# A Strassen MLP on one core: GpSimd's accumulating DMAs moved in layer 0, four output products of each pair deferred into the next pair in layer 1

## The chip, the core and the metric

The kernel runs on one core of a Trainium2 chip. Its time is the device time of one launch in microseconds (us); the runs of the kernel before are given as their median. The core's engines are TensorE (PE; its weight loads are listed as PEld), VectorE (DVE), ScalarE (ACT), GpSimd (POOL) and SyncE (SP), which issues most DMAs. Each has its own queue, works it in order and waits on semaphores.

## The reference

Two layers over 1024 latent and 256 context tokens of width 1024. Layer 0 mixes tokens by a Fourier transform, layer 1 by windowed attention; each mixer is followed by a squared-ReLU MLP with 4096 hidden columns. The change touches the two MLPs alone.

```python
def _sq_relu_mlp(h, w1, w2):
    return jnp.square(jax.nn.relu(h @ w1)) @ w2
...
        h_lat = h_lat + g1 * y_lat
        h_lat = h_lat + g2 * _sq_relu_mlp(_modulate(_rms_norm(h_lat, norm2_g[i]), sh2, sc2), mlp_w1[i], mlp_w2[i])
```

## The kernel before

All matmuls are done in three passes on operands split into a high part (rounded, written by ScalarE) and a low part (what is left, `lo_part`, L58, written by DVE or GpSimd): high by high, low by high, high by low.

Each MLP runs over 16 **pairs** of hidden chunks of 128. In a pair, W1 makes four hidden blocks (B11, B12, B21, B22: two chunks by two halves of 512 tokens), the blocks are squared after ReLU, and W2 takes them back to 1024 rows, kept in `ht`. W2's product is made by Strassen's scheme: seven block products M1 to M7 instead of eight, each of 4 banks with 3 matmuls of 512 columns (12 matmuls). Their right operands are blocks or sums of blocks (T1 to T4), their left ones chunks of W2 or sums of them (S1 to S4). A product lands in four PSUM banks `y_ps` 0 to 3. DVE takes banks 0 to 2 (`acc`: ht += gate * bank). Bank 3 is the side bank: ScalarE copies it, scaled, to `side` (`side_read`), and GpSimd adds it to `ht` (`add`). A bank can be written by the next product only when it has been read.

**Layer 0** (`layer_tail`, L563). Hidden blocks are made directly; after them come M5, M3, M2, M1, M6, M7, M4, with small groups for the context tokens between them (256 columns, bank `l_yc_ps`). The next layer wants sums of its weights. They are made beside this loop, in DRAM: SP copies first terms to `sums` (L825 to L828), and four DMAs a pair on GpSimd's queue add the second terms: `first_sums` (L909, L910), which waits for SP's copies, and `more_sums` for S2 and for S4 (L922), S2 waiting for the first sums to have landed and S4 for S2. GpSimd's own work in a pair (`outputs`) is: addition M5, low part of S2 (of this layer's W2), addition M3, the first sums, the low part of the next pair's first W1 chunk (`low1`), the low part of S3, addition M2, the accumulation for S2, addition M1, the low parts of A22 and A21, the next W1 chunk, additions M6, M7, the accumulation for S4, addition M4. ScalarE splits the W1 chunk (L984, from `l_w1f`) between M1's and M6's side reads. DVE also adds up, from `l_aw`, a part of the modulation of layer 1 (L1288), which a small matmul reduces at the end of the hidden blocks (L1547).

**Layer 1** (`strassen_tail`, L1680). Here the hidden blocks are also made by seven products (M1, M5, M6, M2, M7, M3, M4 on banks `z_ps` 0 to 3, `hidden`), ScalarE copying three of them (`copied`) and DVE adding the copies (`zsum`). Pairs 0 and 1 are plain (hidden blocks directly; in pair 1 the inputs for the later pairs are summed and split, `low_t`); pairs 2 to 15 are alike, 2 to 14 in a loop. TensorE does the seven hidden products and then the seven output products M1, M6, M7, M4, M5, M3, M2. Between the two, DVE and ScalarE must turn hidden blocks into operands: ReLU, square, differences (`diff`), high part (`high`), low part (`low`). A product waits for its operand's low part, its weights' low part (`split2`) and, bank by bank, for the bank's last reader:

```python
                def pair(p):
                    for prod in Z_ORDER:
                        hidden(p, prod)
                    for i in (0, 1, 2, 3):
                        product(p, i)
```

Of the kernel before, what the change touches and what calls it, by code (L numbers as in the profile page):

```python
# [11 lines left out]
P = 128  # L12
# [550 lines left out]
def layer_tail(nc, sem, sb, banks, layer, wp, early, s_pw, w1, w2, mod, meanw, eps, ident, nh, nl, ht,  # L563
# [76 lines left out]
    with ExitStack() as ph:  # L640
# [125 lines left out]
        with nc.Block() as block:  # L766
# [97 lines left out]
            def _(pool):  # L864
# [60 lines left out]
                def outputs(p, more):  # L925
                    add(p, "M5")
                    low2(p, "S2")
                    add(p, "M3")
                    if C:
                        first_sums(p)  # L930
# [17 lines left out]
                    if more and not C:  # L948
                        low1(p + 1, 1)

# [26 lines left out]
                if C:  # L977
                    pool.wait_ge(s_s4, 16 * PAIRS)
# [701 lines left out]
def strassen_tail(nc, sem, sb, banks, wp, early, s_pw, w1, w2, sums, mod, meanw, eps, ident, nh, nl, nl_at, ht, park, out):  # L1680
# [12 lines left out]
    SIDE = 3  # L1693
# [25 lines left out]
    ON_DVE2 = 3  # L1719
    A_ORDER = ["B11", "T2", "T3", "T1", "T4", "B22", "B21"]  # L1720
    A_BUF = {"B11": 0, "B22": 0, "T2": 1, "B21": 1, "T3": 2, "T4": 3, "T1": 4}
    T_AT = {"T1": 1, "T2": 2, "T3": 3, "T4": 4}
    HOME_BANK = {"B21": 0, "B11": 1, "T4": 1, "T3": 2, "B22": 3}
    HOME_SLOT = {"T1": 0, "B12": 1, "T2": 3}
    RELU_SLOT = {"B11": 0, "B12": 1, "B22": 2, "B21": 2}
# [7 lines left out]
    with ExitStack() as ph:  # L1733
# [189 lines left out]
        def split2(eng, p, i):  # L1923
            if i < ON_DVE2:
                eng.wait_ge(s_w2d, p * ON_DVE2 + (PRE + i + 1))
            else:
                eng.wait_ge(s_w2p, p * (7 - ON_DVE2) + (PRE + i - ON_DVE2 + 1))

# [6 lines left out]
        with nc.Block() as block:  # L1935
            @block.sync
            def _(sp):
# [44 lines left out]
                for i in (4, 5, 6):  # L1982
                    load2(0, i, (0, i - 4))
# [5 lines left out]
                load2(1, 0, (0, 4))  # L1989
                load2(1, 1, (0, 5))  # L1990
                load1(2, 3, (1, 3))
                load2(1, 2, (0, 6))

                for i in (4, 5, 6):
                    load2(1, i, (1, i - 4))
                load1(2, 4, (2, 0))
                load1(2, 5, (2, 1))
                load2(2, 3, (1, 3))
                load1(2, 6, (2, 2))
                for i in (0, 1, 2):  # L2000
                    load2(2, i, (1, i + 4))

                with sp.Fori(PLAIN, PAIRS - 1) as p:
                    for i in (4, 5, 6):
                        load2(p, i, (p, i - 4))
                    load1(p + 1, 3, (p, 3))
                    load1(p + 1, 0, (p, 4))
                    load1(p + 1, 1, (p, 5))
                    load1(p + 1, 2, (p, 6))
                    load1(p + 1, 5, (p + 1, 1))  # L2010
                    load1(p + 1, 6, (p + 1, 2))
                    load1(p + 1, 4, (p + 1, 0))
                    load2(p + 1, 3, (p, 3))
                    for i in (0, 1, 2):
                        load2(p + 1, i, (p, i + 4))
                for i in (4, 5, 6):
                    load2(PAIRS - 1, i, (PAIRS - 1, i - 4))
# [9 lines left out]
            def _(pool):  # L2027
# [8 lines left out]
                def low2(p, i):  # L2036
                    pool.wait_ge(s_w2h, p * 7 + (PRE + i + 1))
                    lo_part(pool, w2l[:, i % 3], w2f[:, i % 4], w2h[:, i % 3]).then_inc(s_w2p, 1)

                def add(p, i):  # L2040
                    _, h = chunk(i, SIDE)
                    pool.wait_ge(s_ya, p * 7 + (PRE + i + 1))
                    pool.wait_ge(s_add, p * 7 + (PRE + i))
                    pool.tensor_tensor(h, h, side[i % 2][:], ALU.add).then_inc(s_add, 1)  # L2044
# [7 lines left out]
                def rest(p, more):  # L2052
                    if more:
                        low1(p + 1, 0)
# [1597 lines left out]
```

## Time and profile before

| | us |
|---|---|
| median of 3 runs | 2564.84 (2562.03 to 2565.29) |
| the profiled execution, its own time | 2568.6 |
| its span in the profile | 2567.1 |
| TensorE busy | 2319.5 (90%) |
| DVE busy | 1731.1 (67%) |
| ScalarE, GpSimd busy | 1155.4, 1155.5 (45% each) |

The layer-0 MLP's loop lies between about 410 and 1235 us of the span, the layer-1 MLP's pairs between about 1860 and 2550. Busy time of an engine is counted from instruction starts and ends; matmuls overlap, so TensorE's busy share is close to one also where it works below its pace. PEclk is the granted TensorE clock as a share of full speed. In the waits, the releaser is the operation whose semaphore came last.

### The profile page before, as it was taken

The page shows a single profiled execution, that of the slowest core. Times are in us where ns is not written, and L with a number is a line of the kernel's source. Part 1 is how long each engine was busy: PE and PEld are TensorE (multiplying, and loading weights), DVE is VectorE, ACT ScalarE, POOL GpSimd, SP SyncE. Part 2 cuts the span into 40 slices and gives each one's busy share as a digit, 9 for nine tenths or more (in the row PEclk, how much of TensorE's full clock was granted, in tenths as well). Part 3 has the DMA queues.
Part 4 walks back from the last instruction along what each step waited for, and adds up shares of the span by engine and source line. Part 5 has one row for each costly group of instructions (what it writes and reads, how often), then busy time and mean ns, then how long its engine had stood idle before and what let it go on. Part 6 is the DMA issues. An engine that isn't in the chain of part 4 may idle for free. (4 is left out here: it accounts for less than half of the span.)

```text
span 2567.1 us, 38476 instructions
## 1 busy us (share of the span) xinstructions
PE 2319.5 (90%) x11430; PEld 1908.2 (74%) x11430; DVE 1731.1 (67%) x2827; ACT 1155.4 (45%) x2117; POOL 1155.5 (45%) x974
## 2 busy tenths in 40 slices
PE   5989989999999999999789798989988999998988
PEld 3768768888888877888677677767767777777776
DVE  5643786766776766676674688871787676767675
ACT  5543433333333333333343488883444444444444
POOL 0004533333334444433546566665455554545453
PEclk9999989999999999999889899999989999999999
DMA  7434225555544555554512211105122222222222
GB/s 264 168 136 165 99 60 159 150 139 144 134 131 131 146 144 150 160 151 108 165 61 99 93 32 38 33 21 205 38 66 73 83 82 86 86 86 86 86 80 84
DMA packets 132197, 283.51 MB, mean 110 GB/s; under 512 B 11408, under 2 KB 19984, under 8 KB 128784
## 3 DMA queue, kind: packets, MB, share of 16 engines
q1 hardware_dynamic: 111776, 242.09, 28.1%
q0 software_dynamic: 17408, 33.56, 7.9%
q10 hardware_dynamic: 2928, 6.82, 0.7%
q8 instruction: 43, 0.70, 0.1%
q14 instruction: 42, 0.34, 0.0%
HBM read 265.64 MB, written 83.89 MB: 136 GB/s over the span
## 5 line engine op out<-in xcount | busy, mean ns | idle before, releaser
L881 POOL TENSOR_TENSOR ht<-ht,l_side 128x512 f32<-128x512 f32 x112 | 167.5, 1495 | 535.8 <-ACT l_side L1017 533.6
L51 PE MATMUL l_z_ps<-nh,l_w1h 128*128 128x512 f32 (+1 forms) x816 | 292.9, 359 | 6.6 <-POOL l_w1l L58 3.4
L53 PE MATMUL l_z_ps<-nh,l_w1l 128*128 128x512 f32 (+1 forms) x816 | 291.8, 358 | 0.0
L52 PE MATMUL l_z_ps<-nl,l_w1h 128*128 128x512 f32 (+1 forms) x800 | 285.8, 357 | 0.0
L1321 DVE SCALAR_TENSOR_TENSOR ht<-l_yy_ps,mod,ht 128x512 f32<-128x512 f32 x336 | 235.9, 745 | 20.6 <-PE l_yy_ps L1637 19.2
L2662 PE MATMUL l_yy_ps<-l_ah,l_w2h 128*128 128x512 f32 x448 | 190.2, 425 | 61.3 <-DVE ht L2491 61.1
L58 POOL TENSOR_TENSOR l_w2l<-l_w2f,l_w2h 128x512 fp32r<-128x512 f32 x128 | 181.4, 1467 | 108.9 <-ACT l_w2h L2157 105.1
L58 POOL TENSOR_TENSOR l_w1l<-early,l_w1h 128x512 fp32r<-128x512 f32 x104 | 135.6, 1311 | 179.7 <-ACT l_w1h L2149 179.7
L1635 PE MATMUL l_yy_ps<-l_ah,l_w2h 128*128 128x512 f32 x448 | 187.0, 417 | 22.3 <-ACT l_side L1017 14.6
L3389 POOL TENSOR_TENSOR sc<-sc,den 128x640 f32<-128x640 f32 (+1 forms) x128 | 149.5, 1200 | 91.8 <-DVE den L3471 91.8
L2664 PE MATMUL l_yy_ps<-l_ah,l_w2l 128*128 128x512 f32 x448 | 185.3, 414 | 0.0
L2663 PE MATMUL l_yy_ps<-l_al,l_w2h 128*128 128x512 f32 x448 | 185.3, 414 | 0.0
L1636 PE MATMUL l_yy_ps<-l_al,l_w2h 128*128 128x512 f32 x448 | 182.1, 407 | 0.0
L1637 PE MATMUL l_yy_ps<-l_ah,l_w2l 128*128 128x512 f32 x448 | 180.3, 402 | 0.0
L51 PEld LDWEIGHTS l_z_ps<-nh,l_w1h 128*128 128x128 f32 x816 | 154.8, 190 | 30.4 <-issue 4.0
L2044 POOL TENSOR_TENSOR ht<-ht,l_side 128x512 f32<-128x512 f32 x112 | 151.8, 1355 | 49.5 <-ACT l_side L2194 47.2
L1017 ACT ACTIVATE l_side<-l_yy_ps,mod 128x512 f32<-128x512 f32 x112 | 76.6, 684 | 214.8 <-PE l_yy_ps L1637 214.8
L53 PEld LDWEIGHTS l_z_ps<-nh,l_w1l 128*128 128x128 f32 x816 | 154.9, 190 | 22.4
L52 PEld LDWEIGHTS l_z_ps<-nl,l_w1h 128*128 128x128 f32 x800 | 152.0, 190 | 22.0 <-issue 0.5
L2662 PEld LDWEIGHTS l_yy_ps<-l_ah,l_w2h 128*128 128x128 f32 x448 | 90.1, 201 | 97.1 <-DVE ht L2491 58.4
L2491 DVE SCALAR_TENSOR_TENSOR ht<-l_yy_ps,mod,ht 128x512 f32<-128x512 f32 x192 | 136.3, 745 | 24.2 <-PE l_yy_ps L2664 24.2
L58 DVE TENSOR_TENSOR l_al<-l_slot,l_ah 128x512 fp32r<-128x512 f32 x144 | 119.8, 832 | 37.4 <-ACT l_ah L1010 34.2
(338 smaller groups left out, 6533.5 us busy)
## 6 DMA issues: line engine op xcount, KB each, us to landing
l_aw<-ada SPq DMA_DIRECT2D x128, 256.0 KB, 2.9
sums<-w SPq DMA_DIRECT2D x64, 512.0 KB, 7.8
maw<-ada SPq DMA_DIRECT2D x24, 1024.0 KB, 5.1
l_w1f<-w SPq DMA_DIRECT2D x32, 512.0 KB, 5.8
l_w2f<-w SPq DMA_DIRECT2D x32, 512.0 KB, 4.2
sums<-w POOLq DMA_DIRECT2D x32, 512.0 KB, 7.3
sums<-sums POOLq DMA_DIRECT2D x32, 512.0 KB, 5.9
l_w2f<-sums SPq DMA_DIRECT2D x64, 256.0 KB, 2.7
```

The costliest lines, as they stand in the source:

```text
L51: pe.matmul(out, lh, rh, start=first, stop=False)
L52: pe.matmul(out, lh, rl, start=False, stop=False)
L53: return pe.matmul(out, ll, rh, start=False, stop=last)
L58: return eng.tensor_tensor(lo, full, f32(hi), ALU.subtract)
L881: pool.tensor_tensor(h, h, side[(i - 1) % 2][:], ALU.add).then_inc(s_add, 1)
L1321: dve.scalar_tensor_tensor(out=h, in0=y_ps[m][:], scalar=mod[:, layer, G2, c, 0:1], in1=h, op0=ALU.mult, op1=ALU.add).then_inc(s_acc, 1)
L1635: pe.matmul(y_ps[m][:], wh, a_h, start=first, stop=False, skip_group_check=not first)
L1636: pe.matmul(y_ps[m][:], wh, a_l, start=False, stop=False, skip_group_check=not first)
L1637: pe.matmul(y_ps[m][:], wl, a_h, start=False, stop=True, skip_group_check=not first).then_inc(s_y, 1)
L2662: pe.matmul(y_ps[m][:], wh, a_h, start=start, stop=False, skip_group_check=not start)
L2663: pe.matmul(y_ps[m][:], wh, a_l, start=False, stop=False, skip_group_check=not start)
L2664: pe.matmul(y_ps[m][:], wl, a_h, start=False, stop=True, skip_group_check=not start).then_inc(s_y, 1)
```

## The change

**Layer 0.** GpSimd's four accumulating DMAs get other places in `outputs`. The first sums of pair p come first of all, behind the S4 accumulation of pair p − 1; S2's comes after the last addition. After the last pair S4's follows at once.

**Layer 1.** Output products 3 to 6 (M4, M5, M3, M2) of pair p − 1 are done among the hidden products of pair p: after hidden M1, M5, M6, and after the last one (M4). M1, M6, M7 of pair p follow. All five queues are rewritten to suit: the order of operands becomes B11, T2, T3, B21, T4, T1, B22; two low parts of W2 more are on DVE and fewer on GpSimd; copies and buffers change places; and of the first and the last output product (M1 and M2) two banks, 2 and 3, go by ScalarE and GpSimd instead of one. T2 and B21 share an operand buffer, as before, so the high part of T2 now waits for the output product M2 of the pair before.

```diff
                 def outputs(p, more):
+                    if C:
+                        if type(p) is not int or p:
+                            more_sums(p - 1, "S4")
+                        first_sums(p)
                     add(p, "M5")
                     low2(p, "S2")
                     add(p, "M3")
-                    if C:
-                        first_sums(p)
...
                     for prod in ROWS[2:]:
                         add(p, prod)
-                        if C and prod in ("M2", "M7"):
-                            more_sums(p, "S2" if prod == "M2" else "S4")
...
+                    if C:
+                        more_sums(p, "S2")
...
                 outputs(PAIRS - 1, False)
                 if C:
+                    more_sums(PAIRS - 1, "S4")
                     pool.wait_ge(s_s4, 16 * PAIRS)
...
-    A_ORDER = ["B11", "T2", "T3", "T1", "T4", "B22", "B21"]
+    A_ORDER = ["B11", "T2", "T3", "B21", "T4", "T1", "B22"]
+    A_AFTER = {"B11": (1, 5), "B22": (0, 0), "T2": (1, 6), "B21": (0, 1), "T1": (1, 4)}
+    SIDES = {i: [2, 3] if i in (0, 6) else [3] for i in range(7)}
...
-                def pair(p):
-                    for prod in Z_ORDER:
+                def pair(p, earlier=True):
+                    for k, prod in enumerate(Z_ORDER):
                         hidden(p, prod)
-                    for i in (0, 1, 2, 3):
+                        if earlier and k < 3:
+                            product(p - 1, 3 + k)
+                    if earlier:
+                        product(p - 1, 6)
+                    for i in (0, 1, 2):
                         product(p, i)
```

DVE's queue in a pair of layer 1, from the last difference on:

```diff
+                    diff(p, "T1")
+                    diff(p, "T2")
+                    if earlier:
+                        acc(p - 1, 6, (0, 1))
+                    square(p, "B21")
+                    if earlier:
+                        acc(p - 1, 6, (2, 3))
+                    low(p, "T2")
+                    acc(p, 0, (0,))
+                    diff(p, "T3")
+                    acc(p, 0, (1, 2, 3))
+                    low(p, "T3")
+                    diff(p, "T4")
+                    acc(p, 1, (0, 1))
+                    low(p, "B21")
+                    acc(p, 1, (2, 3))
+                    low(p, "T4")
+                    acc(p, 2)
```

In the second plain pair DVE's low parts of T4 leave their place before `last_sums` and follow the accumulation of the sixth product (`plain_rest`).

How the order moves on GpSimd, in the first pair of layer 0 (L881 the additions, L58 low parts, L909 and L910 the first sums, L922 S2 or S4). Before:

```order
L881 TENSOR_TENSOR ht0<-ht0,l0_side0 128x512
L58 TENSOR_TENSOR l0_w2l<-l0_w2f,l0_w2h 128x512
L881 TENSOR_TENSOR ht0<-ht0,l0_side1 128x512
L909 DMA sums<-w1 128x2x512
L910 DMA sums<-w2 128x2x512
L58 TENSOR_TENSOR l0_w1l<-l0_w1f,l0_w1h 128x1024
L58 TENSOR_TENSOR l0_w2l<-l0_w2f,l0_w2h 128x512
L881 TENSOR_TENSOR ht0<-ht0,l0_side0 128x512
L922 DMA sums<-sums 128x2x512
L881 TENSOR_TENSOR ht0<-ht0,l0_side1 128x512
L58 TENSOR_TENSOR l0_w2l<-l0_w2f,l0_w2h 128x512 x2
```

And with the change:

```order
L909 DMA sums<-w1 128x2x512
L910 DMA sums<-w2 128x2x512
L881 TENSOR_TENSOR ht0<-ht0,l0_side0 128x512
L58 TENSOR_TENSOR l0_w2l<-l0_w2f,l0_w2h 128x512
L881 TENSOR_TENSOR ht0<-ht0,l0_side1 128x512
L58 TENSOR_TENSOR l0_w1l<-l0_w1f,l0_w1h 128x1024
L58 TENSOR_TENSOR l0_w2l<-l0_w2f,l0_w2h 128x512
L881 TENSOR_TENSOR ht0<-ht0,l0_side0 128x512
L881 TENSOR_TENSOR ht0<-ht0,l0_side1 128x512
L58 TENSOR_TENSOR l0_w2l<-l0_w2f,l0_w2h 128x512 x2
```

No DMA is left between the first addition and the two low parts.

On ScalarE, in the last pair of layer 1, from the ReLU of the last hidden block (slot2 from z_ps0) on; l1_ah is a high part (of T2 from slot3, of T3 from z_ps2, of T1 from slot0, of T4 and B21 from z_ps1 and z_ps0), l1_side a side read, l1_w2h a split of W2. Before:

```order
L2177 ACTIVATE l1_slot2<-l1_z_ps0 128x512
L2188 ACTIVATE l1_ah<-l1_slot3 128x512
L2188 ACTIVATE l1_ah<-l1_z_ps2 128x512
L2188 ACTIVATE l1_ah<-l1_slot0 128x512
L2194 ACTIVATE l1_side0<-l1_yy_ps3,mod 128x512
L2157 ACTIVATE l1_w2h<-l1_w2f 128x512
L2188 ACTIVATE l1_ah<-l1_z_ps1 128x512
```

And with the change:

```order
L2217 ACTIVATE l1_slot2<-l1_z_ps0 128x512
L2230 ACTIVATE l1_ah<-l1_slot3 128x512
L2238 ACTIVATE l1_side1<-l1_yy_ps2,mod 128x512
L2238 ACTIVATE l1_side0<-l1_yy_ps3,mod 128x512
L2230 ACTIVATE l1_ah<-l1_z_ps2 128x512
L2195 ACTIVATE l1_w2h<-l1_w2f 128x512
L2238 ACTIVATE l1_side0<-l1_yy_ps2,mod 128x512
L2238 ACTIVATE l1_side1<-l1_yy_ps3,mod 128x512
L2195 ACTIVATE l1_w2h<-l1_w2f 128x512
L2230 ACTIVATE l1_ah<-l1_z_ps0 128x512
```

Two side reads of the pair before stand between T2's and T3's high parts, and two of this pair behind T3's; T1's high part (slot0) has moved further back.

## Rows read from the trace of the kernel before

**Rows 1.** Waits of the whole run: who waited for whom, us in total, times, longest.

```profile
PE l_yc_ps L51 <- POOL l_w2l L58: 32.4, 15, 4.7
...
PE l_yy_ps L2662 <- DVE ht L2491: 61.1, 33, 6.2
```

**Rows 2.** Timeline of TensorE, one layer-0 pair: start, duration, line, operation [idle before].

```profile
705.26 0.95 PE L1547 MATMUL l_yc_ps<-ones,l_side 128*128 128x1 f32 x8
...
725.72 0.50 PE L1635 MATMUL l_yy_ps<-l_ah,l_w2h 128*128 128x512 f32 x1 [0.79 <-ACT l_side L1017]
...
728.70 0.51 PE L51 MATMUL l_yc_ps<-l_ach,l_w2h 128*128 128x256 f32 x1 [2.02 <-POOL l_w2l L58]
...
731.36 0.63 PE L1635 MATMUL l_yy_ps<-l_ah,l_w2h 128*128 128x512 f32 x1
...
734.51 0.28 PE L51 MATMUL l_yc_ps<-l_ach,l_w2h 128*128 128x256 f32 x1
...
735.94 0.40 PE L51 MATMUL l_z_ps<-nh,l_w1h 128*128 128x512 f32 x1
...
763.50 0.95 PE L1547 MATMUL l_yc_ps<-ones,l_side 128*128 128x1 f32 x8
```

**Rows 3.** Windows: stretch, length, busy PE, PEld, DVE, ACT, POOL, PEclk, DMA share, GB/s.

```profile
730.00:732.00 2.00, 2.00 (x10) 1.90 (x9) 0.40 (x1) 0.00 (x0) 1.97 (x2) 0.50 0.91 331
```

**Rows 4.** Windows over the 14 looped pairs of layer 0 and 13 of layer 1.

```profile
413.40:1233.86 820.46, 778.12 (x3979) 665.01 (x3978) 567.91 (x910) 269.44 (x447) 321.81 (x238) 0.97 0.53 142
1962.69:2531.44 568.75, 525.65 (x2184) 419.93 (x2184) 385.31 (x547) 261.61 (x453) 302.55 (x233) 0.97 0.27 82
```

**Rows 5.** Timeline of GpSimd in the same layer-0 pair.

```profile
723.52 1.15 POOL L922 DMA_DIRECT2D sums<-sums  x1 [2.16 <-DMA sums<-w]
...
725.52 2.90 POOL L58 TENSOR_TENSOR l_w2l<-l_w2f,l_w2h 128x512 fp32r<-128x512 f32 x2
```

**Rows 6.** Timeline of ScalarE there.

```profile
724.03 1.06 ACT L984 ACTIVATE l_w1h<-l_w1f 128x1024 fp32r<-128x1024 f32 x1 [2.70 <-DMA l_w1f<-w]
725.00 0.67 ACT L1017 ACTIVATE l_side<-l_yy_ps,mod 128x512 f32<-128x512 f32 x1
```

**Rows 7.** Timeline of TensorE, one layer-1 pair: first hidden matmul, then the output products.

```profile
2114.47 0.39 PE L2645 MATMUL l_z_ps<-nh,l_w1h 128*128 128x512 f32 x1
...
2133.72 0.40 PE L2662 MATMUL l_yy_ps<-l_ah,l_w2h 128*128 128x512 f32 x1
...
2137.67 0.49 PE L2662 MATMUL l_yy_ps<-l_ah,l_w2h 128*128 128x512 f32 x1 [1.02 <-DVE ht L2491]
...
2141.65 0.64 PE L2662 MATMUL l_yy_ps<-l_ah,l_w2h 128*128 128x512 f32 x1 [2.32 <-DVE ht L2491]
```

**Rows 8.** Timeline of DVE in the same layer-0 pair: sums over l_aw.

```profile
754.16 0.75 DVE L1288 SCALAR_TENSOR_TENSOR l_side<-l_aw,l_sseq,l_side 128x512 f32<-128x512 f32 x1 [0.80 <-DMA l_aw<-ada]
...
760.02 1.65 DVE L1288 SCALAR_TENSOR_TENSOR l_side<-l_aw,l_sseq,l_side 128x512 f32<-128x512 f32 x2
```

**Rows 9.** Timeline of DVE in the first pair of layer 0.

```profile
357.47 6.33 DVE L1314 TENSOR_TENSOR l_slot<-l_slot 128x512 f32<-128x512 f32 x2
```

**Rows 10.** Timeline of GpSimd at the end of layer 0 and the next stage.

```profile
1267.94 1.27 POOL L887 TENSOR_TENSOR sqs<-sqs 128x512 f32<-128x512 f32 x1
1271.76 0.56 POOL L2919 MEMSET vs<- 128x256 f32 x2 [2.55 <-POOLq L76]
```

**Rows 11.** The line of S2's and S4's accumulations, L922: issue to landing.

```profile
DMA to landing us min/median/max: 5.2/5.9/11.4
```

**Rows 12.** Timeline of DVE in the pair of rows 7.

```profile
2136.11 0.68 DVE L58 TENSOR_TENSOR l_al<-l_z_ps,l_ah 128x512 fp32r<-128x512 f32 x1
2136.71 1.40 DVE L2491 SCALAR_TENSOR_TENSOR ht<-l_yy_ps,mod,ht 128x512 f32<-128x512 f32 x2
...
2139.43 1.50 DVE L58 TENSOR_TENSOR l_al<-l_slot,l_ah 128x512 fp32r<-128x512 f32 x1
```

**Rows 13.** Timeline of DVE, second plain pair of layer 1: low parts of T4.

```profile
1904.17 5.95 DVE L2438 SCALAR_TENSOR_TENSOR nl<-l_nf,nh 128x512 fp32r<-128x512 f32 x4
```

More of the change, by code:

```diff
@@ L2070, in pair @@
                         low1(p + 1, 2)
-                    rest(p, more)
+                        low1(p + 1, 0)
+                    if earlier:
+                        add(p - 1, 6)
+                    low2(p, 2)
+                    add(p, 0)
+                    low2(p, 3)
+                    add(p, 1)
+                    low2(p, 4)
+                    add(p, 2)
                 def low_p(w):
@@ L2318, in _ @@
                     side_read(0, i)
-                for i in (0, 1, 2):
-                    high2(1, i)
+                high2(1, 1)
+                high2(1, 0)
                 relu(1, "B11")
@@ L2332, in _ @@
                 high(1, "T3")
-                high(1, "T1")
+                high2(1, 2)
                 side_read(1, 0)
@@ L2348, in _ @@
                     high_t("T3", j)
-                side_read(1, 3)
-                high2(1, 6)
                 for i in (4, 5, 6):
                     side_read(1, i)
-                with act.Fori(PLAIN, PAIRS - 1) as p:
-                    start(p, True)
-                    rest(p, True)
-                    for i in (4, 5, 6):
-                        side_read(p, i)
+                pair(PLAIN, True, False)
+                with act.Fori(PLAIN + 1, PAIRS - 1) as p:
+                    pair(p, True)
                 last = PAIRS - 1
-                start(last, False)
-                rest(last, False)
+                pair(last, False)
+                high2(last, 6)
+                side_read(last, 3)
+                high2(last, 5)
                 def out_half(i):
@@ L2506, in last_sums @@
-                    low(p, "T4")
-                    acc(p, 1, 0)
+                    acc(p, 2)
                     low(p, "B22")
-                    acc(p, 1, 1)
-                    acc(p, 1, 2)
-                    acc(p, 2, 0)
-                    low(p, "B21")
-                    acc(p, 2, 1)
-                    acc(p, 2, 2)
-                    for i in (3, 4, 5, 6):
-                        for m in range(3):
-                            acc(p, i, m)
-                        if side_sums and i < 5:
-                            for j in range(HK):
-                                low_t("T1" if i == 3 else "T3", j)
@@ new lines, in plain_rest, with pair_start @@
+                    acc(p, 6)
+                def pair_start(p):
+                    low(p - 1, "T1")
+                    acc(p - 1, 3)
+                    low2(p - 1, 6)
+                    low(p - 1, "B22")
+                    low2(p - 1, 5)
+                    acc(p - 1, 4)
+                def pair(p, earlier=True):
+                    if earlier:
+                        pair_start(p)
+                    low2(p, 1)
+                    if earlier:
+                        acc(p - 1, 5)
+                    low2(p, 0)
@@ L2582, in _ @@
                 square(1, "B22")
-                for j in range(HK):
-                    low_t("T4", j)
-                last_sums(1, True)
-                with dve.Fori(PLAIN, PAIRS) as p:
+                plain_rest(1)
+                pair(PLAIN, False)
+                with dve.Fori(PLAIN + 1, PAIRS) as p:
                     pair(p)
+                pair_start(PAIRS)
+                acc(PAIRS - 1, 5)
+                acc(PAIRS - 1, 6)
                 for i in range(len(HALVES)):
@@ L2704, in _ @@
                     product(1, i)
-                for t in ("T1", "T2", "T3", "T4"):
-                    pe.wait_ge(s_tlo[t], HK)
-                with pe.Fori(PLAIN, PAIRS - 1) as p:
+                pair(PLAIN, False)
+                with pe.Fori(PLAIN + 1, PAIRS - 1) as p:
                     pair(p)
-                    for i in (4, 5, 6):
-                        product(p, i)
                 pair(PAIRS - 1)
+                product(PAIRS - 1, 3)
                 for n in range(3):
```

329 lines of the change are left out of this document (193 added, 136 removed).

## The prediction, made before the change ran

> **What bounds the kernel now.** I took the list of waits first, because TensorE is busy nearly all the time and only its waits can be won. Two waits come back in every pair of hidden chunks [rows 1]: in layer 0 TensorE waits 15 times for a low part made on GpSimd (32.4 us in all); in layer 1 its output matmuls wait 33 times for DVE's accumulation into ht (61.1).
>
> Then the timeline of one layer-0 pair. TensorE stands idle for 0.79 and, two matmuls later, for 2.02 us [rows 2]; its granted clock then falls to 0.50, the lower level of 1.2 GHz [rows 3]. The price of that: the twelve narrow matmuls of the context group take 731.36 − 728.70 = 2.66 us, where twelve alike take 735.94 − 734.51 = 1.43 [rows 2]. So this pair loses 0.79 + 2.02 + 1.23, and some 0.8 more in restarts and in two wide matmuls still at the lower clock: 4.8 us. This pair lasts 763.50 − 705.26 = 58.2 us, the 14 looped pairs 820.46 / 14 = 58.60 on average [rows 2, 4]; a pair with none of this is thus 53.4, and the mean loss 5.2.
>
> Who is late? GpSimd, after its addition for M2, stands idle 2.16 us, from 721.4, until the DMA of the first sums has landed, issues S2's accumulation, and reaches the two low parts that TensorE wants only at 725.52 [rows 5]. ScalarE is blocked by a weight load: it waits 2.70 us for l_w1f, and the side read that TensorE needs follows at 725.00, behind the split [rows 6].
>
> In layer 1 the looped pairs last 568.75 / 13 = 43.75 us [rows 4]. The seven hidden products, 84 matmuls, run without a gap from 2114.47 to 2133.72, 0.229 us each [rows 7]; 168 of them make 38.5, so 5.2 is lost. After the first output product TensorE idles 1.02 us, and two banks later 2.32, both for DVE [rows 7], and the mean granted clock of the stretch is 0.97 [rows 4]. The reason is order: after the last hidden product DVE must finish squares, differences and low parts, and only 12 matmuls of M1's output cover it.
>
> **The change, part by part.** (1) Layer 0, GpSimd's queue. S2 and S4 leave the middle of the output stage, the first sums leave the place before low1; all four DMAs of a pair now stand where GpSimd has nothing to do until the next pair's first side read, a whole stage of hidden blocks later. Their issue, 1.15 us for S2's [rows 5], is covered by that idle time. In the frame of rows 5: GpSimd ends the addition for M2 at 721.4, less 1.5 for the first sums gone, takes M1's addition as soon as its side read is there, and needs 1.3 for it and 2.5 for the two low parts: done by about 724, where TensorE comes at 725.6. The 2.02 goes. The l_w1f load is issued some 1.5 us earlier and no longer beside 1 MB of accumulating DMAs; ScalarE's split should end before M6's last bank is written, so the 0.79 goes, and with both the fall of the clock. Floor 53.4. What is late next is the sum over l_aw, by DVE: its loads now share the DMA engines with S4 and the first sums. DVE already waits 0.80 for one of them, and the last two steps run from 760.02 to 761.7, against TensorE's need at 763.5, so there is slack of 1.8 us [rows 2, 8]. I charge 0.5 a pair: gain 4.7, by 14 pairs 66 us. Bounds: 2.2 (only the GpSimd wait goes, the rest comes back as a wait for l_aw) and 5.2, so 31 to 73.
>
> (2) First pair of layer 0: a DVE operation with both inputs in SBUF waits some 5 us while GpSimd issues the first sums and works on [rows 9]. Without the issues there I take 2 us (0 to 5).
>
> (3) End of layer 0: S2 and S4 of the last pair now stand behind the last addition. Before, GpSimd's last operation ends at 1269.2 and the next stage begins at 1271.8 [rows 10]. Now two accumulations follow one after the other, each landing after 5.9 us (5.2 at best) plus its issue [rows 11]; GpSimd's last operation comes some 6 us earlier by (1), at 1263.2, and 2 × (0.7 + 5.9) follow: 1276.4, or 7.2 later than before; with the 5.2 of the best landings 5.8. I take a cost of 6 (3 to 10).
>
> (4) Layer 1, TensorE's order: four output products of pair p − 1 are put between and behind the hidden products of p. M2's output (12 matmuls, 2.75 us) now stands between the last hidden product and M1's output, so DVE's chain has 24 matmuls of cover. I lay the pair out from its start at 0, with 2.75 per product: last hidden product ends 27.5, M2's output 30.2, then M1 to 33, M6 to 35.7, M7 to 38.5. DVE's accumulation takes 0.70 and a low part 0.68 [rows 12]; ScalarE's side read 0.67 [rows 6]. T1 and T2 are ready at 28.3. But T2's high part shares a buffer with B21 of the pair before and must wait for M2's output, to 30.8, and on ScalarE the two side reads of M2 queue behind it, to 32.1, then T3's high part, W2's split and M1's two side reads, to 35.4: bank 2 of M6's output finds its bank unread for about 0.5. DVE goes low T2 31.5, accumulation, T3, accumulation, low T3 34.3, T4, two accumulations 36.4; then low B21, which waits for M6's output to end (same buffer), 37.6, and only then bank 2 of M6, 38.3, which M7's output wants at 37.5: 0.8. With 0.4 for one DVE operation held up by GpSimd (next part) the period is 38.5 + 0.5 + 0.8 + 0.4 = 40.2; gain 3.55 by 13 pairs = 46 us. Neither idle is as long as the 2.32 after which the clock fell, so I charge no lower clock. Bounds: 39.0 and 42.0, that is 62 to 23 us. If M2's cover were gone, the old 1.02 and 2.32 would be back. The extra side bank in the first and last product takes two of DVE's 21 accumulations (1.4 us) and gives ScalarE 1.4 and GpSimd 2 × 1.3 more, on engines with over 15 us free. The loads on SP are reordered, each still a product or more ahead: nothing.
>
> (5) GpSimd against DVE. DVE's low part of T1, two inputs in SBUF, took 1.50 instead of 0.68 beside GpSimd [rows 12]; GpSimd now works almost without a break from 28.6 to 42.7, beside the low parts of T2 and T1. I take half of one such delay on the path, 0.4. The Trainium skill ("SBUF — State Buffer", section "SBUF: two separate sides") calls the port pair shared by the two an exclusive lock held for a whole instruction, also when DVE has two SBUF inputs and GpSimd reads SBUF. That rule speaks against this change: by it each of the two low parts can lose a full GpSimd operation. The trace agrees in kind (1.50 against 0.68), with 0.82 lost; by the rule the sum would be that of rival B, 2474.
>
> (6) Second plain pair of layer 1: the four low parts of T4, 5.95 us on DVE, stood ahead of what TensorE waited 6.2 us for, the longest of its 33 waits [rows 1, 13]; they move behind the sixth product's accumulation. Gain 5 (3 to 6). The first looped pair gains 1; two additions in a row at the very end cost 0.6.
>
> **The sum:** 66 + 2 − 6 + 46 + 5 + 1 − 0.6 = 113 us. The profiled execution took 2568.6 us (span 2567.1), 3.8 above the median of 2564.84; 2568.6 − 113.4 = 2455.2 on its scale, and 2451 against the median.
>
> **The rivals.** A. Layer 0 gives it back: the accumulating DMAs slow the l_aw loads by 2 us each, DVE comes late, TensorE waits where the modulation is reduced. For it: slack is only 1.8. Against: DMA demand there is light. Price: layer 0 gains 31 instead of 66, 2486.
> B. GpSimd's additions hold DVE up in layer 1: an addition there lasts 1.27 [rows 10], two low parts a pair lose one each, 2.5 instead of 0.4 on the path; period 42.3, some of it covered, so 42.0: gain 23 instead of 46, 2474. For it: the 1.50. Against: only one such delay per pair now.
> C. Slower. GpSimd's unbroken run keeps DVE out for as long as in the first pair, 5 us at a time [rows 9], for both T2 and T1: 40.2 + 10 = 50.2, so 13 × 6.45 = 84 us lost where 46 were gained: 2451 + 130 = 2581. It turns the sum from 113 / 13 = 8.7 us of blocking a pair on. Against: the longest such hold in the layer-1 loop was 0.8.
> D. Better: layer 0 runs at its floor (7 more) and layer 1 at 39.0 (16 more), 2428. E. The DMA order changes nothing since something else, l_w1f's load, holds ScalarE anyway: layer 0 gains 25, 2492.
>
> **How the numbers follow.** Forecast 0.50, A 0.12, B 0.20, C 0.03, D 0.08, E 0.07. Predicted 2451; the range from 2424 (near D) to 2500 takes in A, B and E and leaves C and the tails out. Differences below 0.2% (5 us) can't be told from none here. Faster 0.95, same 0.02, slower 0.03.
>
> **What would show it.** Layer-0 pairs 53.4 to 54.5 us apart with no wait of l_yc_ps for GpSimd's l_w2l and PEclk 1.00 there; the next stage beginning about 11 us after GpSimd's last addition of layer 0; layer-1 pairs 39.5 to 41 apart, their remaining waits at the third bank of M6's and M7's outputs, for ScalarE's side read and DVE's ht. I am wrong if TensorE waits for DVE's l_side sum in layer 0, or if a layer-1 pair stays above 42.

## The result and the profile after

| | before | after |
|---|---|---|
| median of 5 runs, us | 2565.29 (2562.03 to 2568.72) | 2547.19 (2540.97 to 2551.47) |
| ratio, 95% interval | | 0.9924 [0.9901, 0.9947] |
| span of the profiled execution | 2567.1 | 2549.9 |

The change gains 0.8%, 18 us, where 113 were forecast and the slow end of the range was 2500. All launches of this document lie within 0.5% of their kernel's median but one of kernel 12, which took 4607 us and is left out of its ratio. The spans differ by 17.2 us. Both spans are divided at the same places: the first matmul of the reductions of pairs 1 and 15 of layer 0, the next stage's first matmul, and the first matmul of what follows the attention (its output projection, then layer 1's MLP):

| stretch | before | after | difference |
|---|---|---|---|
| up to the reduction of pair 1 | 413.4 | 414.7 | +1.3 |
| 14 looped pairs of layer 0 | 820.5 | 838.2 | +17.7 |
| last reduction to the next stage's first matmul | 37.9 | 45.7 | +7.8 |
| attention stage | 465.5 | 466.4 | +0.9 |
| from there to the end (projection and layer 1's MLP) | 829.7 | 784.85 | −44.9 |

Layer 1 delivers nearly what was forecast. Layer 0 has become slower: a pair takes 838.2 / 14 = 59.9 us, not 53.9.

The waits of the whole run, TensorE's, after the change (who waited for whom, us in total, times, longest):

```profile
PE l_yc_ps L1550 <- DVE l_side L1291: 55.9, 14, 5.1
PE l_yy_ps L2753 <- DVE ht L2544: 22.3, 25, 2.7
PE qkv_ps L3270 <- PEq L76: 15.2, 1, 15.2
...
PE l_yy_ps L1638 <- DVE ht L1324: 8.9, 5, 3.3
PE l_yy_ps L2753 <- ACT l_side L2238: 5.7, 13, 0.6
```

The wait for GpSimd's l_w2l [rows 1] is gone, with all its 32.4 us. Layer 1's wait for DVE fell from 61.1 [rows 1] to 22.3. But a wait that no row of before has stands on top: the reduction in layer 0 waits 14 times (pairs 1 to 14), 4.0 us on average, for DVE's sum over l_aw. And this is what DVE waits for:

```profile
DVE l_side L1291 <- DMA l_aw<-ada: 100.6, 30, 6.7
```

Before, the same 30 waits made 19.9 us:

```profile
DVE l_side L1288 <- DMA l_aw<-ada: 19.9, 30, 0.9
```

The timeline of DVE in one looped pair shows where they lie in the changed kernel (start, duration, line, operation, idle before):

```profile
759.30 0.75 DVE L1291 SCALAR_TENSOR_TENSOR l_side<-l_aw,l_sseq,l_side 128x512 f32<-128x512 f32 x1 [0.21 <-DVE l_side L1291]
...
766.57 0.75 DVE L1291 SCALAR_TENSOR_TENSOR l_side<-l_aw,l_sseq,l_side 128x512 f32<-128x512 f32 x1 [5.28 <-DMA l_aw<-ada]
769.48 0.75 DVE L1291 SCALAR_TENSOR_TENSOR l_side<-l_aw,l_sseq,l_side 128x512 f32<-128x512 f32 x1 [2.15 <-DMA l_aw<-ada]
...
774.13 1.64 DVE L1291 SCALAR_TENSOR_TENSOR l_side<-l_aw,l_sseq,l_side 128x512 f32<-128x512 f32 x2
```

The last step ends at 775.77, and TensorE was free for it at 771.60. Two steps were late for their rows (5.28, then 2.15); six operations on blocks follow on DVE before the last two steps, which are thus late for the queue. GpSimd's timeline of the same pair says what was moving then:

```profile
744.73 1.14 POOL L922 DMA_DIRECT2D sums<-sums  x1
756.90 1.14 POOL L922 DMA_DIRECT2D sums<-sums  x1 [11.03 <-issue]
757.71 1.40 POOL L909 DMA_DIRECT2D sums<-w  x1
758.40 1.87 POOL L910 DMA_DIRECT2D sums<-w  x1
```

S2's accumulation goes out behind the last addition, as intended. GpSimd then runs straight on into the next pair's head, waits 11 us for S2 to land, and issues S4's accumulation and both first sums at 757 to 758: nothing but S2's landing holds them. SyncE issues this pair's six loads of l_aw from 753.7 on, into two buffers: the third and fourth of them can start only when the DVE steps of 758.34 and 759.30 have freed these, at 759.1 and 760.1, just behind the first sums. They are the two that come late. The third is issued at 759.25:

```profile
759.25 0.33 SPq L791 DMA_DIRECT2D l_aw<-ada  x1
DMA to landing us min/median/max: 7.2/7.2/7.2
```

The fourth, issued at 760.21, takes 9.0 us; the third of the pair shown before, issued at 751.31, took 2.7. In windows (stretch, length, busy PE, PEld, DVE, ACT, POOL, PEclk, DMA share, GB/s) the same place after (first) and before (second) the change:

```profile
757.70:768.00 10.30, 10.30 (x47) 8.52 (x47) 3.62 (x6) 2.35 (x4) 2.57 (x3) 1.00 0.97 182
```

```profile
750.00:762.00 12.00, 12.00 (x60) 10.15 (x59) 9.80 (x16) 4.77 (x8) 0.00 (x0) 1.00 0.29 87
```

The 16 DMA engines are full (0.97) where they were at 0.29. Over the whole run an l_aw load lands after 3.7 us in the median and 9.9 at worst, where it was 2.9 and 6.2.

The wait is not the whole price. TensorE, having stood for 4.3 us, starts again at the lower clock:

```profile
771.32 0.28 PE L53 MATMUL l_z_ps<-nh,l_w1l 128*128 128x256 f32 x1
775.90 1.07 PE L1550 MATMUL l_yc_ps<-ones,l_side 128*128 128x1 f32 x8 [4.30 <-DVE l_side L1291]
776.83 0.78 PE L1638 MATMUL l_yy_ps<-l_ah,l_w2h 128*128 128x512 f32 x1
777.40 0.63 PE L1639 MATMUL l_yy_ps<-l_al,l_w2h 128*128 128x512 f32 x1
```

After it the wide matmuls stand 0.43 us apart instead of 0.23 up to 779.96; one pair earlier this lasted from 716.0 to 722.1. The window that begins at that earlier reduction has PEclk 0.58, between the levels of 1.2 and 2.4 GHz:

```profile
714.80:723.00 8.20, 8.20 (x26) 6.72 (x27) 5.04 (x10) 1.88 (x4) 0.09 (x1) 0.58 0.00 0
```

26 matmuls were done in these 8.2 us; the kernel of experiment 3, without the wait, does 43 in the 8.2 us from its reduction on (below). 17 × 0.23 = 3.9 us are lost to the clock and the restart in this pair. Over the 14 looped pairs the granted clock is 0.95:

```profile
414.72:1252.92 838.20, 785.87 (x3977) 674.92 (x3978) 567.16 (x912) 266.19 (x446) 328.46 (x236) 0.95 0.52 138
```

**Layer 1** came out where the prediction laid it. One looped pair, TensorE:

```profile
2234.48 0.50 PE L2753 MATMUL l_yy_ps<-l_ah,l_w2h 128*128 128x512 f32 x1 [0.43 <-ACT l_side L2238]
...
2238.20 0.50 PE L2753 MATMUL l_yy_ps<-l_ah,l_w2h 128*128 128x512 f32 x1 [0.70 <-DVE ht L2544]
```

These two answer to the 1.02 and the 2.32 of [rows 7]. They stand at bank 2 of M6's and of M7's output. From ScalarE's side reads 12 periods apart, a pair takes 40.85 us (43.78 before).

### The profile page after: what moved, and what is told of

It reads as the page before. It is cut to its first block and busy times, and to the rows that moved or that the text cites. A ratio compares the mean times of both kernels' runs of the same rounds, so it can differ in the third digit from the quotient of the medians.

```text
span 2549.9 us, 38622 instructions
## 1 busy us (share of the span) xinstructions
PE 2314.1 (91%) x11430; PEld 1899.3 (74%) x11430; DVE 1741.3 (68%) x2811; ACT 1169.6 (46%) x2149; POOL 1192.9 (47%) x990
## 3 DMA queue, kind: packets, MB, share of 16 engines
q0 software_dynamic: 17408, 33.56, 7.8%
## 5 line engine op out<-in xcount | busy, mean ns | idle before, releaser
L881 POOL TENSOR_TENSOR ht<-ht,l_side 128x512 f32<-128x512 f32 x112 | 147.8, 1320 | 403.5 <-ACT l_side L1020 399.9
L1324 DVE SCALAR_TENSOR_TENSOR ht<-l_yy_ps,mod,ht 128x512 f32<-128x512 f32 x336 | 236.7, 745 | 31.5 <-PE l_yy_ps L1640 30.6
L2080 POOL TENSOR_TENSOR ht<-ht,l_side 128x512 f32<-128x512 f32 x144 | 198.6, 1379 | 84.0 <-ACT l_side L2238 78.0
L58 POOL TENSOR_TENSOR l_w1l<-early,l_w1h 128x512 fp32r<-128x512 f32 x104 | 136.9, 1324 | 180.3 <-ACT l_w1h L2188 180.3
L2753 PE MATMUL l_yy_ps<-l_ah,l_w2h 128*128 128x512 f32 x448 | 185.7, 415 | 29.0 <-DVE ht L2544 22.3
L1013 ACT ACTIVATE l_ah<-l_slot 128x512 fp32r<-128x512 f32 x112 | 70.6, 630 | 215.6 <-DVE l_slot L1303 109.5
L1291 DVE SCALAR_TENSOR_TENSOR l_side<-l_aw,l_sseq,l_side 128x512 f32<-128x512 f32 x112 | 87.0, 777 | 109.4 <-DMA l_aw<-ada 100.6
L58 DVE TENSOR_TENSOR l_al<-l_slot,l_ah 128x512 fp32r<-128x512 f32 x144 | 125.7, 873 | 50.3 <-ACT l_ah L1013 40.3
L58 DVE TENSOR_TENSOR l_w2l<-l_w2f,l_w2h 128x512 fp32r<-128x512 f32 x128 | 119.6, 936 | 51.0 <-ACT l_w2h L2195 39.8
```

The costliest lines, as they stand in the source:

```text
L58: return eng.tensor_tensor(lo, full, f32(hi), ALU.subtract)
L1324: dve.scalar_tensor_tensor(out=h, in0=y_ps[m][:], scalar=mod[:, layer, G2, c, 0:1], in1=h, op0=ALU.mult, op1=ALU.add).then_inc(s_acc, 1)
L2080: pool.tensor_tensor(h, h, side[k % 2][:], ALU.add).then_inc(s_add, 1)
L2753: pe.matmul(y_ps[m][:], wh, a_h, start=start, stop=False, skip_group_check=not start)
```

## The experiments

Theory: the accumulating DMAs of layer 0, moved to where GpSimd has nothing to do, run beside the l_aw loads and make them late; DVE's sum, TensorE and its clock follow. Layer 1 is independent of that. Rivals: the loss in layer 0 comes from layer 1's part; the l_aw loads are late for another reason; wherever these DMAs go, some other load will be late instead.

"Change" is the changed kernel (2547), "gated" the third kernel here (2451). Ratios are to the kernel before, measured beside each. It took 2565.1 beside kernels 1 to 4, 2563.4 beside 6 to 9, and 2565.4 beside 5 and 10 to 12. A difference of 6 or 7 us between kernels of different groups is thus only just clear of the noise; the periods of the pairs carry these readings. In kernels with the same order they repeat to 0.03 us in layer 1, and in layer 0 with the gate (without it, to 0.4).

**1 and 2. Each part alone.** First the change with layer 0's `outputs` as before; second the kernel before with the change's `outputs`:

```diff
 # 1, on the change (2: the reverse, on the kernel before)
-                    if C:
-                        if type(p) is not int or p:
-                            more_sums(p - 1, "S4")
-                        first_sums(p)
                     add(p, "M5")
                     low2(p, "S2")
                     add(p, "M3")
+                    if C:
+                        first_sums(p)
...
+                        if C and prod in ("M2", "M7"):
+                            more_sums(p, "S2" if prod == "M2" else "S4")
...
-                    if C:
-                        more_sums(p, "S2")
...
-                    more_sums(PAIRS - 1, "S4")
```

> The changed kernel with layer 0's GpSimd order put back as it was before: layer 1's part alone. Theory (the layers add, layer 0's part costs time through late l_aw rows): layer-0 loop pairs 58.6 us apart again (820.5 us over 14, against 838.2 in the changed kernel), end of layer 0 about 37.9 us instead of 45.7, so 1.3 + 17.7 + 7.8 = 27 us less than the changed kernel: about 2520 us, ratio to the kernel before about 0.982; layer-1 pairs 40.8 us apart. Rival (layer 1's part itself slows layer 0, for instance through buffers or placement): layer-0 pairs stay near 59.9 us and the time near 2547 us.

Measured: 2519.2 us, ratio 0.9821 [0.9796, 0.9846]; layer-0 pairs 821.3 / 14 = 58.7, layer-1 pairs 40.84.

> The kernel before with layer 0's GpSimd order of the change: layer 0's part alone. Theory: slower than before by 27 us, about 2592 us, layer-0 pairs 59.9 us apart with TensorE waiting 3 to 5 us at the reduction for DVE's l_side sum, layer-1 pairs 43.75 us apart as before. Rival (layer 0's loss comes only together with layer 1's part): within 5 us of 2565 us.

Measured: 2588.2 us, ratio 1.0085 [1.0063, 1.0107]; layer-0 pairs 832.3 / 14 = 59.5, TensorE waiting 14 times for l_side, 52.3 us in all. The parts add: 2519.2 − 2565.1 = −45.9 for layer 1, +23.1 for layer 0, −22.8 together, where the change gave −18. The loss is layer 0's own, and the first rival falls.

**3. The gate.** GpSimd may issue the sums of a pair only when DVE has done its last l_aw step:

```diff
                     if C:
+                        pool.wait_ge(s_as, p * STEPS + (PRE + STEPS))
                         if type(p) is not int or p:
                             more_sums(p - 1, "S4")
                         first_sums(p)
```

> The changed kernel with one wait added: at the head of a pair's outputs GpSimd waits for DVE's last sum over l_aw rows before it issues S4's sum and the two first sums, so that these DMAs start only when the l_aw rows are in. Theory (these DMAs delay the l_aw rows, those the DVE sum, that TensorE, whose clock then starts low): no wait for l_side at the reduction above 0.5 us, DVE's waits for l_aw near 20 us in total instead of 100.6, outputs matmuls 0.23 us from the first on, layer-0 pairs 53.4 to 54.5 us apart, total 2547 - 14 x (59.9 - 54) = about 2465 us (2455 to 2480). Rival 1 (the l_aw rows are late for another reason, such as SyncE's queue starting them later, or S2's sum alone, still issued at 744.7 us in the pair): l_aw waits stay above 60 us, total within 10 us of 2547. Rival 2 (the sums only move to l_w1f or l_w2f, whose loads then come late and hold ScalarE): l_side wait gone, but pairs 56 to 58 us apart, total 2495 to 2520.

Measured: 2450.95 us, ratio 0.9556 [0.9537, 0.9575]. That is better than the expected 2455 to 2480. Layer-0 pairs 746.9 / 14 = 53.35, each within 0.1 of it. The wait for l_side is gone from TensorE's list, and DVE's list says

```profile
DVE l_side L1292 <- DMA l_aw<-ada: 19.1, 30, 0.9
```

TensorE's timeline runs over the reduction without a gap, and the window behind it has the full clock, though the sums now fill the DMA engines right there (share 0.89):

```profile
729.96 0.28 PE L53 MATMUL l_z_ps<-nh,l_w1l 128*128 128x256 f32 x1
730.08 0.95 PE L1551 MATMUL l_yc_ps<-ones,l_side 128*128 128x1 f32 x8
730.89 0.47 PE L1639 MATMUL l_yy_ps<-l_ah,l_w2h 128*128 128x512 f32 x1
```

```profile
730.10:738.30 8.20, 8.20 (x43) 6.91 (x42) 6.34 (x11) 4.17 (x8) 5.88 (x6) 1.00 0.89 147
```

So it isn't the amount of DMA work but what stands beside it. GpSimd waits 25 us at the gate and loses nothing, since the side read for its first addition of the pair is there only at 735.31. The other two rivals fall: nothing else delays the l_aw rows, and no other load becomes late enough to cost a pair anything.

**4 and 5. Which of the sums.** In the fourth kernel the first sums go back behind M3's addition, S4 stays at the head; in the fifth the gate stands between S4 and the first sums.

```diff
 # 4, on the change
-                    if C:
-                        if type(p) is not int or p:
-                            more_sums(p - 1, "S4")
-                        first_sums(p)
+                    if C and (type(p) is not int or p):
+                        more_sums(p - 1, "S4")
...
                     add(p, "M3")
+                    if C:
+                        first_sums(p)
 # 5, on the change
                             more_sums(p - 1, "S4")
+                        pool.wait_ge(s_as, p * STEPS + (PRE + STEPS))
                         first_sums(p)
```

> The changed kernel with the two first sums issued behind the addition of M3, where they were before; S4's sum stays at the head of the outputs (it is issued at about 757 us in the pair, beside the l_aw loads) and S2's at their end. Theory, the large first sums being the main part of the collision: the DVE sum late by under 1.5 us instead of 3 to 5, pairs 54 to 56 us apart, total about 2480 us (2460 to 2500). Rival (S2 and S4, not the first sums, slow the l_aw rows): pairs 58 to 60 us apart, total 2530 to 2550.

Measured: 2471.0 us, ratio 0.9629 [0.9608, 0.9651]; pairs 54.6. DVE waits 30.3 us for l_aw, TensorE not at all for l_side, but 14 times for ScalarE's side read, 13.7 us in all: with the first sums behind M3 a pair still takes 1.3 more than the gated kernel's 53.35.

> The gated kernel with S4's sum ahead of the gate, so that it runs beside the l_aw rows while the two first sums still wait. Theory (the first sums are the main part of the collision): DVE's waits for l_aw 25 to 45 us instead of 19, no more than 0.5 us at the reduction, layer-0 pairs 53.4 to 54 us apart, 2451 to 2460 us. Rival (S4's sum alone is enough to make the l_aw rows late): pairs 56 or more, above 2485 us.

Measured: 2455.4 us, ratio 0.9562 [0.9541, 0.9584]; pairs 53.35, waits for l_aw 26.3 us. S4 beside the l_aw loads costs the pairs nothing that the runs can tell, though those waits are 7 us longer than with the gate ahead of it. The collision needs the two first sums. Whether they would do it alone is open: in the change they follow right behind S4's accumulation, and land after 9.4 and 12.0 us in the median; in this kernel, away from it, after 6.3 and 8.3. They were not run beside the l_aw loads without it.

**6. Bytes or accumulation?** On the change, the two first sums as plain writes. This kernel leaves the addition out, so layer 1 computes with other weights.

```diff
-...accum_op=ALU.add, max_dma_last_dim=2048).then_inc(s_s1, 16)
+...max_dma_last_dim=2048).then_inc(s_s1, 16)     (both DMAs of first_sums)
```

> The changed kernel (no gate) with the two first sums issued as plain writes, without accumulation, so that layer 1's deferred products are computed from other weights; order, sizes and queue as in the changed kernel. Theory that the bytes moved beside the l_aw rows are what delays them: still two writes of 512 KB at the same moment, so the DVE sum stays late by 2 us or more, layer-0 pairs 57 to 60 us apart, total 2510 to 2547 us. Rival (accumulation, with its read of the destination, is what makes them slow): the first sums land in 6 us or less, layer-0 pairs 54 to 56 us apart, total 2465 to 2490 us.

Measured: 2502.6 us, ratio 0.9765 [0.9748, 0.9782], pairs 791.7 / 14 = 56.5, landings of 6.6 and 8.0 us in the median (9.4 and 12.0 with accumulation), waits for l_aw 72.0 us, TensorE's for l_side 29.1 (2.1 a pair). It lies between the two: of the 6.5 us a pair that the collision costs, 3.3 go with the accumulation and 3.2 stay for the plain writes. Neither expectation was right. The profiled launch is the fastest of the four, 10 us below their median; by the medians 44.6 us go of the 96.2 that the gate gives back, so about half in either count. The queue moves the same 33.56 MB, but in 13312 packets instead of 17408: the addition itself and the number of packets are not told apart here.

**7. The end of layer 0.** On the gated kernel, in the last pair alone:

```diff
                         add(p, prod)
+                        if C and not more and prod in ("M2", "M7"):
+                            more_sums(p, "S2" if prod == "M2" else "S4")
...
-                    if C:
+                    if C and more:
                         more_sums(p, "S2")
...
-                    more_sums(PAIRS - 1, "S4")
```

> The gated kernel with the last pair of layer 0 alone changed: S2's and S4's sums behind the additions of M2 and M7 as before, in place of behind the last addition. Theory (GpSimd waits there for S2's landing, then S4's, after its last addition, and the next stage starts behind it): last reduction to next stage's first TensorE instruction about 38 us instead of 45.4, total 2443 to 2445 us. Rival (the next stage waits for something else): no change, 2449 to 2453 us.

Measured: 2443.6 us, ratio 0.9529 [0.9516, 0.9543], 7.3 below the gated kernel. From the last reduction to the next stage's first matmul it is 35.4 us instead of 45.4 (37.9 in the kernel before). GpSimd in the changed kernel, at that end:

```profile
1284.06 1.26 POOL L887 TENSOR_TENSOR sqs<-sqs 128x512 f32<-128x512 f32 x1
1285.27 1.18 POOL L922 DMA_DIRECT2D sums<-sums  x1
1291.42 1.15 POOL L922 DMA_DIRECT2D sums<-sums  x1 [4.97 <-DMA sums<-sums]
1298.58 0.56 POOL L3012 MEMSET vs<- 128x256 f32 x2 [6.01 <-POOLq L76]
```

and in this kernel, where both sums went out long before (S4's at 1183.92):

```profile
1188.97 1.71 POOL L887 TENSOR_TENSOR sqs<-sqs 128x512 f32<-128x512 f32 x1
1192.44 0.56 POOL L3014 MEMSET vs<- 128x256 f32 x2 [1.76 <-POOLq L76]
```

13.3 us from the end of GpSimd's last operation to the next stage have become 1.8. Of the 10 us won on TensorE there, 5.7 arrive in the span of the profiled launches: in this one the attention stage took 1.0 more and the stretch behind it 3.1 more than in the gated kernel's, with the same code and the same periods of the looped pairs, and the start up to pair 1 took 0.2 more. No cause of that shows.

**8. Layer 1: one side bank.** On the gated kernel:

```diff
-    SIDES = {i: [2, 3] if i in (0, 6) else [3] for i in range(7)}
+    SIDES = {i: [3] for i in range(7)}
```

> The gated kernel (2451 us) with layer 1's side path taking only bank 3 of every product, so that DVE adds bank 2 of the first and the last product too. Theory (the second bank takes about 1.5 us of DVE work per pair off the path that TensorE waits for): layer-1 pairs 41.3 to 42.3 us apart instead of 40.8, total +7 to +20 us, 2458 to 2471. Rival (DVE has slack there and the side path's own waits of 0.4 us vanish instead): pairs 40.3 to 40.8 apart, total 2444 to 2452.

Measured: 2443.5 us, ratio 0.9531 [0.9515, 0.9547]; pairs 40.05 against 40.83. The rival held: with the second side bank a pair is 0.8 slower. Without it TensorE has no wait for ScalarE's side read, and one of 0.34 for DVE.

**9. Layer 1: one row of DVE's order.** On the gated kernel, whose M6 addition of bank 2 stands behind the low part of B21:

```diff
                     diff(p, "T4")
-                    acc(p, 1, (0, 1))
+                    acc(p, 1)
                     low(p, "B21")
-                    acc(p, 1, (2, 3))
                     low(p, "T4")
```

> The gated kernel with one row of layer 1's DVE order moved: both last additions of M6's output (banks 2 and 3 as far as DVE has them) ahead of the low part of B21. Theory (the 0.7 us wait at the third bank of M7's output is DVE's addition of M6's bank 2, queued behind that low part, which itself waits 1.15 us for ScalarE): the wait goes, layer-1 pairs 40.1 to 40.4 us apart, total 2442 (2440 to 2447). Rival (the low part of B21 comes late for its product in place of it): pairs 40.8 or more, total 2449 to 2455.

Measured: 2440.7 us, ratio 0.9516 [0.9503, 0.9529]; pairs 39.86, a little better than the theory's 40.1. The rows on DVE, in the gated kernel

```profile
2216.59 0.69 DVE L58 TENSOR_TENSOR l_al<-l_z_ps,l_ah 128x512 fp32r<-128x512 f32 x1 [1.14 <-ACT l_ah L2231]
2217.20 0.74 DVE L2545 SCALAR_TENSOR_TENSOR ht<-l_yy_ps,mod,ht 128x512 f32<-128x512 f32 x1
```

and here

```profile
2210.69 2.08 DVE L2545 SCALAR_TENSOR_TENSOR ht<-l_yy_ps,mod,ht 128x512 f32<-128x512 f32 x3
2213.25 0.69 DVE L58 TENSOR_TENSOR l_al<-l_z_ps,l_ah 128x512 fp32r<-128x512 f32 x1 [0.48 <-ACT l_ah L2231]
```

The addition no longer stands behind a low part that waits 1.14 us for ScalarE; TensorE's 0.70 is gone. The 0.43 for the side read is still there.

**10 to 12. Together.** The gate, 7 and 9 in one kernel, with the side banks as in the change, with one, and with two in the first product alone:

```diff
 # 10
     SIDES = {i: [2, 3] if i in (0, 6) else [3] for i in range(7)}
 # 11
-    SIDES = {i: [2, 3] if i in (0, 6) else [3] for i in range(7)}
+    SIDES = {i: [3] for i in range(7)}
 # 12
-    SIDES = {i: [2, 3] if i in (0, 6) else [3] for i in range(7)}
+    SIDES = {i: [2, 3] if i in (0,) else [3] for i in range(7)}
```

> The gated kernel with both the moved DVE row of layer 1 and the earlier S2 and S4 sums of layer 0's last pair; two side banks in the first and last product as in the change. The two steps lie in different stages, so they should add: 2451 - 10.3 - 7.3 = 2433 us (2431 to 2436), layer-1 pairs 39.85 us apart. Rival (they share a limit): 2438 or more.

Measured: 2430.9 us, ratio 0.9473 [0.9455, 0.9490]; layer-1 pairs 39.85. They add.

> The same as c1 with the side path taking bank 3 alone in every product. Theory (the second bank's reads and additions make GpSimd's additions late for the two side buffers, TensorE's wait of 0.43 us for ScalarE's side read, and hold DVE up by shared use; DVE has room for the two additions): layer-1 pairs 39.3 to 39.7 us apart, total 2425 to 2431 us. Rival (with the row moved, DVE's two further additions are what ends last): pairs 40 us apart, total 2434 to 2438 us.

Measured: 2431.3 us, ratio 0.9475 [0.9457, 0.9492]; pairs 39.65, TensorE waiting 0.32 for DVE. The period is in the theory's range and the time at its slow edge; the rival falls. But the pairs are only 0.2 better than in kernel 10, and the times don't differ: once the row is moved, two banks in both products cost next to nothing.

> The same as c1 with two side banks only in the first block product and one in the last. Theory (the 0.43 us wait is the side buffer that GpSimd's addition of the last product's second bank frees late, the others of the two additions cost little): the wait goes, pairs 39.3 to 39.6 us apart, 2425 to 2430 us. Rival (the wait is the first product's own two reads): it stays, pairs 39.8 us or more, 2432 to 2436 us.

Measured: 2427.4 us, ratio 0.9459 [0.9443, 0.9476]; pairs 39.45, as the theory had it. Neither the wait for the side read nor the one for DVE is left in the looped pairs. In kernel 10, as in the change, ScalarE waits 4.2 us in all for GpSimd's additions, which free the two side buffers; with the last product's second bank left to DVE that wait has left the list. This is the fastest version, 5.4% below the kernel before; its interval overlaps those of 10 and 11, and only the profiled periods set it apart. A third side buffer, another way to free that read, was not tried.

## Why the prediction was wrong

**Term (1), layer 0, failed.** Its first half was right. Both waits of [rows 2] went, GpSimd's low parts are in time, and the floor of 53.4 is real: the gated kernel runs at 53.35. The step that failed is the charge of 0.5 us a pair for the late l_aw sum. It measured 59.87 − 53.35 = 6.5 us a pair, 91 over the loop, which turned a gain of 73 into a loss of 18. A wait of TensorE for DVE's l_side sum was the sign that the prediction itself named for being wrong. Three things were wrong in it.

The slack of 1.8 us was read from a stretch in which the DMA engines were at 0.29. I named the DMAs that would come there and didn't lay them out against the loads. The issue times could have been had from the rows at hand: S2 leaves behind the last addition, S4 waits for its landing (5.9 at the median, 11.4 at worst [rows 11]) and nothing further holds the first sums, so they start 6 to 12 us after the last addition, with DVE's steps over l_aw [rows 8] and their loads right behind. The median hides the case that counts: behind SyncE's five copies and loads S2 now lands after 10.1 to 11.3 us in 14 of the 16 pairs, and S4's accumulation, which stood there before, had taken 9.8 to 11.4 in as many. I called the place one "where GpSimd has nothing to do", which is a statement about GpSimd's queue, not about the DMA engines or about what SyncE does there.

The lower bound of 2.2 a pair assumed that at most 3.0 comes back. There was no reason for it; the bound should have been taken with no excuse from l_aw, and it would have been below nothing.

And nothing was charged for the clock behind a wait of 4 us. The waits inside the loop make (55.9 − 3.5) / 14 = 3.7 a pair (the first of the 14, 3.5 us, lies ahead of it); the rest of the 6.5, 2.8, is the lower clock behind them: a granted clock of 0.953 over the 838.2 us of the loop is 39 us, 2.8 a pair, and TensorE has no other wait there. [rows 2, 3] had shown this effect, and I charged it to the wait that was to go, not to the one that could come.

**Rival A was the mechanism**, with 12% and with 2486 for a price. It too was undersized: it took 2 us for each late load, where the two shown took 7.2 and 9.0 us to land instead of some 2.9, and nothing for the clock.

**Terms (2) and (3).** The first pair's wait of 5.26 us fell to 3.29, 2.0 as forecast, and DVE's long pair of differences there from 6.33 [rows 9] to 4.38; but this pair, too, ends in the new wait, so the loop starts 1.3 later rather than 2 earlier. The end of layer 0 cost 7.8 where 6 (3 to 10) was forecast. The accumulations behind GpSimd's last operation were to take 13.2, and the next stage began 13.3 after it (the "about 11 us" among the signs doesn't fit that sum). But GpSimd's last operation ended only 3.0 us earlier than before, 32.4 instead of 35.4 after the last reduction, and not 6. Experiment 7 gave 7.3 of it back.

**Term (4), layer 1, was right in its places and a little large.** Forecast 40.2 a pair, measured 40.85: 13 × 2.93 = 38 us instead of 46. The stalls stood at the banks named, 0.43 for 0.5 and 0.70 for 0.8. What was missing is what a stop costs beyond its wait: the matmul behind the 0.43 starts 0.83 after the one before, the one behind the 0.70 1.09 after, each with a further 0.34 behind it, where 0.23 is the pace; four more starts nearby come 0.31 to 0.46 apart. Together they are 2.2 over 38.5. "Nothing" for the extra side bank was wrong: experiment 8 measured 7.5 us for it, 0.8 a pair (0.2 once DVE's row is moved, experiment 11). I had counted busy time on ScalarE and GpSimd, which is indeed free, and not that the two side buffers tie the read of one product to GpSimd's addition for the one before.

**Term (5).** The low parts of T2 and T1 lasted 1.04 and 1.32 us instead of 0.68, 1.0 together for the 0.82 seen before; no hold of 5 us came back, so rival C is out, and rival B's 2.5 a pair is far too much. (Its 1.27 for an addition is a row of another operation, L887; layer 1's additions took 1.36 on average.) How much of the 1.0 lay on the path was not measured by itself.

**Term (6).** TensorE's waits of 6.24 and 3.91 us in the second plain pair are gone; the longest there is 1.96. Of the 44.9 us that the last stretch gained, 38 are the looped pairs, so 6.7 are left for this and the ends, against 5 + 1 − 0.6 = 5.4.

**The sum.** Forecast 66 + 2 − 6 + 51 = 113; measured −17.7 − 1.3 − 7.8 − 0.9 + 44.9 = 17.2. Put the gate in, and the same kernel takes 2450.95. That this is the forecast of 2451 to the decimal is luck: layer 0's loop then gives 73.5 instead of 66, and layer 1 less than was forecast.

## What to carry to other kernels

A DMA has two places: that in the queue which issues it, and that on the DMA engines. Moving it to where its issuing engine is free says nothing about the second. Work out when it will start (what is the last thing that holds it?) and list the loads that another queue issues in the following 10 us, and how close to being needed each of them is. If a late place is wanted and the queue can't give it, one wait for the consumer of the loads at risk gives it: here one line was worth 96 us. And where TensorE may come to wait for some us, price the matmuls behind the wait at the lower clock too.

## What was not expected of the hardware

The two first sums of 512 KB each, with S4's just ahead of them and the l_aw loads between, filled the 16 DMA engines to 0.97 at only 182 GB/s, where the loop before reached 331 GB/s at 0.91 [rows 3] in a stretch of SyncE's loads without an accumulation under way. Issued as plain writes, they landed after 6.6 us instead of 9.4 in the median (the first of the two), and about half of the loss was gone. Two 256 KB loads issued just behind them took 7.2 and 9.0 us to land (the median before was 2.9). And a sum of 512 KB alone (S4) beside the same loads left the period of the pairs at 53.35.
